# Latent tokens: both expert tables streamed once per latent step in place of gathered rows

## What is computed

```python
def peer_ffn(h, lp):
    q = (xt @ lp["peer_wq"]).reshape(n_tok, PEER_HEADS, 2, PEER_HALF)
    s = jnp.einsum("thmd,mhnd->thmn", q, lp["peer_keys"])
    v1, i1 = lax.top_k(s[:, :, 0], PEER_TOPK)
    v2, i2 = lax.top_k(s[:, :, 1], PEER_TOPK)
    ...
    idx = jnp.take_along_axis(cand_i, pos, axis=-1)    # i1 * 128 + i2, of 16384 experts
    g = jax.nn.softmax(top_s, axis=-1)
    act = jnp.einsum("td,thkd->thk", xb, u_tab[ib])
    return jnp.einsum("thk,thkd->td", jax.nn.gelu(act) * gb, v_tab[ib])
```

## Time and profile before

| | |
|---|---|
| median of 3 runs | 2433.51 us (2430.46 to 2434.32) |
| span of the profiled execution | 2689.8 us |
| TensorE, VectorE, ScalarE, GpSimd busy | 1510.1, 1524.4, 281.3, 1466.1 us |
| moved by DMA | 969.43 MB, mean 360 GB/s |
| granted TensorE clock, mean | 0.721 |

### The profile page before, as it was taken

How to read it: one execution, slowest core, us unless ns; L and a number is a source line. 1 busy time by engine, 2 the same in 40 slices (tenths; PEclk the granted TensorE clock), 3 DMA queues, 4 the chain that set the end, 5 groups by cost and what they waited for, 6 DMA issues and landing times.

```text
span 2689.8 us, 20637 instructions
## 1 busy us (share of the span) xinstructions
PE 1510.1 (56%) x6676; PEld 682.0 (25%) x6676; DVE 1524.4 (57%) x4059; ACT 281.3 (10%) x715; POOL 1466.1 (55%) x1540
## 2 busy tenths in 40 slices
PE   6898668694244554554556866868400444442466
PEld 2464433371012110122312442354100100110012
DVE  0349974756886555455360965575776844446401
ACT  1321133010000110100000032211000000000000
POOL 0005445536665666666556635545676666667664
PEclk8889888896666665676768787878755655565568
DMA  9979998988999999999979988888899999999997
GB/s 360 411 320 379 395 388 324 365 306 318 357 397 411 412 388 379 371 410 411 389 286 374 364 341 314 324 313 296 318 399 373 343 383 375 358 374 383 378 357 271
DMA packets 238044, 969.43 MB, mean 360 GB/s; under 512 B 26314, under 2 KB 28746, under 8 KB 227954
## 3 DMA queue, kind: packets, MB, share of 16 engines
q0 software_dynamic: 221184, 805.40, 78.0%
q1 hardware_dynamic: 16754, 162.71, 14.9%
HBM read 964.87 MB, written 3.15 MB: 360 GB/s over the span
## 4 chain that ended last, share of the span: by engine, by line
DVE 27%; PE 24%; issue 15%; POOL 13%; another core or an unknown queue 11%; DMA 7%; ACT 2%; SPq 0%; DVEq 0%; ACTq 0%; POOLq 0%
PE acc L1077 8%; PE psum L1031 6%; DVE ring L1871 6%; POOL work L695 6%; POOL ring L695 5%; DVE work L1871 3%; PE psum L786 3%; DVE work L1463 2%; POOL wring L695 2%; DMA ring<-peer_v_in,vidx 2%; PE psum L796 2%; DVE work L1460 2%; DMA ring<-peer_u_in,idx 1%; DVE wring L1871 1%
## 5 line engine op out<-in xcount | busy, mean ns | idle before, releaser
L695 POOL DMA_INDIRECT ring<-peer_u_in,idx x415 | 396.5, 955 | 460.6 <-DVE idx L1566 208.0
L1871 DVE CUSTOM_DVE_ANT_0 ring<-ring,h_kept 128x1024 f32<-128x1024 f32 x415 | 488.9, 1218 | 126.3 <-DMA ring<-peer_u_in,idx 93.5
L695 POOL DMA_INDIRECT ring<-peer_v_in,vidx x392 | 378.5, 966 | 325.8 <-PE acc L1077 116.9
L1077 PE MATMUL acc<-ring,vw 128*32 128x512 f32 x1412 | 299.2, 778 | 276.6 <-DVE vw L1852 107.6
L1077 PE MATMUL acc<-work,vw 128*32 128x512 f32 x852 | 218.4, 794 | 325.5 <-DVE vw L1852 155.0
L1871 DVE CUSTOM_DVE_ANT_0 work<-work,h_kept 128x1024 f32<-128x1024 f32 x220 | 262.0, 1219 | 159.3 <-DMA work<-peer_u_in,idx 124.2
L695 POOL DMA_INDIRECT work<-peer_v_in,vidx x267 | 252.0, 944 | 144.8 <-issue 74.0
L695 POOL DMA_INDIRECT work<-peer_u_in,idx x220 | 207.1, 941 | 116.7 <-issue 58.9
L1031 PE MATMUL psum<-work,wring 128*128 128x256 f32 (+1 forms) x896 | 187.1, 369 | 49.5 <-issue 46.6
L786 PE MATMUL psum<-wring,work 128*128 128x512 f32 (+1 forms) x432 | 180.4, 575 | 32.4 <-issue 22.8
L1031 PEld LDWEIGHTS psum<-work,wring 128*128 128x128 f32 x896 | 160.3, 216 | 81.5 <-issue 62.0
(11 more groups left out here) (244 smaller groups left out, 2028.4 us busy)
## 6 DMA issues: line engine op xcount, KB each, us to landing
wring<-w_in_in SPq DMA_DIRECT2D x17, 2048.0 KB
wring<-peer_wq_in SPq DMA_DIRECT2D x14, 2048.0 KB
wring<-mod_w_in SPq DMA_DIRECT2D x10, 2048.0 KB
ring<-mod_w_in SPq DMA_DIRECT2D x9, 2048.0 KB, 12.2
wring<-w_out_in SPq DMA_DIRECT2D x8, 2048.0 KB
work<-mod_w_in SPq DMA_DIRECT2D x5, 2048.0 KB, 14.4
ring<-peer_u_in,idx POOLq DMA_INDIRECT x415
ring<-peer_v_in,vidx POOLq DMA_INDIRECT x392
```

Source lines behind the costliest of these rows:

```text
L695: nc.gpsimd.indirect_dma_start(slots[slot_of[n]], None, table, bass.IndirectOffsetOnAxis(ap=at[:, col + r:col + r + 1], axis=0))\
L1077: ins = mm(acc[half][lane:lane + QUAD, :], w[:, at:at + QUAD], two[j - pair][0][:, half * CHUNK:(half + 1) * CHUNK], start=(r == 0), stop= ...
L1871: V.tensor_tensor_reduce(held, held, h_kept[:, :], 1.0, 0.0, ALU.mult, ALU.add, dots[:, dots_at(k, t) + r:dots_at(k, t) + r + 1]).then_inc ...
```

## The change

For the latent steps (k = 1 and 3) the gathers are replaced. For the context steps they stay.

1. `laid_out` gives both tables in a second layout: 64 parts of U and 64 of V per layer, each 128 partitions x 8 KB (1 MB). Expert n * 128 + m lies on "partition n, column m"; a part holds two columns m, so a pass covers 256 experts. The U part is transposed, so that its 128x128 blocks can be weights.
2. After the last `choose` of a latent step comes a new generator, `dense_gates`. Per tile, the picks' row numbers, column numbers and gates are transposed (`pickT`). Then, per group of four tokens, VectorE writes two one-hot matrices [128 picks, 128] (one weighted by the gates), TensorE multiplies them for each token into a 128x128 matrix of gates, and ScalarE carries them into a staging tile. After eight groups ScalarE sends the tile to the main memory (2 MB, eight times per step). The calculation of `idx` and the regrouping to `vidx` are left out for latent steps; `idx` and `vidx` hold the two halves as floats.
3. The events of a latent step are now `p`, `w`, `m`, 64 of each, and one `x`. `p`: GpSimd loads a part of U (direct DMA); TensorE multiplies 16 times (two columns of experts x 8 blocks, 256 moving columns: both tiles of tokens) into a bank; ScalarE applies gelu into one of 7 buffers. `w`: VectorE multiplies by the dense gates, of which GpSimd loads a slice of 1 MB every four passes. `m`: GpSimd loads a part of V; TensorE multiplies 8 times (two columns x two tiles x two halves of 512) into `acc` for tile 0 and `h_kept` for tile 1. `p` runs five passes ahead of `m`, `w` two.
4. 85% of these events are spread by weight over all pauses of the context step behind; the rest, and all of step 3's, come after the dense work. Nothing but the gates' own work is at the new pauses.
5. Parts use the ten places of the ring as five, and at the end four more in the weight ring. The lent places beside and behind the context layouts are gone, those of `hn`, `mod_g2` and `mod_norms` stay. `ahead` is off for all steps. Step 2 waits for the stores of the gates ahead of some of its buffers, where it waited for `picked`.

The sizes, and the loads on GpSimd:

```diff
+PAIR = 2
+PASSES = 128 // PAIR
+LEAD, READY = 5, 2
+SLOTS = 5
+SLICE = 4
+GROUP = 32
...
-                self.ahead = k == 3
+                self.ahead = False
...
+            def load_part(kind, k, c):
+                to, landed, _ = part(kind, k, c)
+                slot, n = part_at(kind, k, c), part_no[kind, k, c]
+                if n - part_first[k] >= part_slots(k):
+                    pool.wait_ge(*part_left(slot, k, n))
...
+                nc.gpsimd.dma_start(to, io["u_parts" if kind == "p" else "v_parts"][k // 2, c]).then_inc(landed, 16)
```

TensorE:

```diff
+            def dense_gates(st):
...
+                    for q in range(P // 4):
+                        p = job(pe, "G", k, t, q)
+                        pe.wait_ge(*after("hot", k, t, q))
+                        hot = st.L.onehot[q % 2]
+                        for u in range(4):
+                            ins = mm(p[:, u * P:(u + 1) * P], hot[:, u * P:(u + 1) * P], hot[:, 512 + u * P:512 + (u + 1) * P],
+                                     start=True, stop=True)
+            def experts(kind, k, c):
+                if kind == "p":
...
+                    for j in range(PAIR):
+                        for b in range(DB):
+                            ins = mm(p[:, j * 256:(j + 1) * 256], w[:, b, j * P:(j + 1) * P], st.L.hT[1][:, b, 0:256],
+                                     start=(b == 0), stop=(b == DB - 1))
...
+                    for j in range(PAIR):
+                        for t in range(2):
+                            for half in range(2):
+                                ins = mm(sum_of(t, half), w[:, j * 256 + t * P:j * 256 + (t + 1) * P],
+                                         rows_of[:, j, half * CHUNK:(half + 1) * CHUNK],
+                                         start=(c == 0 and j == 0), stop=(c == PASSES - 1 and j == PAIR - 1))
```

ScalarE:

```diff
+                        carry(stage.rearrange("p (n t) -> p t n", t=GROUP)[:, q % 8 * 4:q % 8 * 4 + 4, :],
+                              bank("G", k, t, q)[:, :].rearrange("p (t n) -> p t n", t=4), "G", k, t, q)
+                        if q % 8 == 7:
+                            act.wait_ge(*taken("G", k, t, q))
+                            act.dma_start(io["dense_gates"][st.layer, g], stage).then_inc(*mark(stored, k, g, n=16))
...
+                    A(acts[c % len(acts)], bank("act", k, c)[:, :], ACT.Gelu_apprx_tanh).then_inc(*take("act", k, c))
```

VectorE:

```diff
+                        for u in range(4):
+                            n = 4 * q + u
+                            d(V.tensor_scalar(hot[:, u * P:(u + 1) * P], c("count"), picks[:, n:n + 1],
+                                              picks[:, 2 * P + n:2 * P + n + 1], ALU.is_equal, ALU.mult))
+                        wide = [P, 4, P]
+                        V.tensor_tensor(hot[:, 512:1024].rearrange("p (u n) -> p u n", u=4), c("count").unsqueeze(1).broadcast_to(wide),
+                                        picks[:, P + 4 * q:P + 4 * q + 4].unsqueeze(2).broadcast_to(wide), ALU.is_equal)\
+                            .then_inc(*mark("hot", k, t, q))
...
+                    V.tensor_tensor(w, w, g[:, first:first + PAIR, :, :], ALU.mult).then_inc(*mark("wt", k, c))
```

The plan:

```diff
+def expert_events(st):
+    events = []
+    for c in range(-LEAD, PASSES):
+        for kind, at in (("p", c + LEAD), ("w", c + READY), ("m", c)):
+            if 0 <= at < PASSES:
+                events.append((kind, st.k, 0, at))
+    return events + [("x", st.k, 0, 0)]
...
+BESIDE_SHARE = 0.85
...
         elif k and k < len(steps):
-            dots = max(n for n, event in enumerate(left) if event[0] == "u") + 1
-            most = dots + int((len(left) - dots) * ROOM)
-            spread(plan, part(names[0][0], ("wq", 3)), left[:dots])
-            spread(plan, part(("ps", 0), ("exp", 0)), left[dots:most])
+            most = int(len(left) * BESIDE_SHARE)
+            spread(plan, names, left[:most])
             plan[None] = left[most:]
```

More of the change, by code:

```diff
@@ L344, in mod_column @@
             return columns_of[:, at:at + 1]
-        def dots_at(k, t):
-            return (sum(st.T for st in steps[:k]) + t) % 2 * PICKS
-        vw_places = [held[:, :] for held in vw] + [region(16384 + i * CHUNK, CHUNK) for i in range(2)]
         def vw_of(k, t, q):
-            return vw_places[q % (4 if k == STEPS - 1 else 2)]
+            return vw[q % 2][:, :]
         def job(pe, *key):
@@ L471, in spare @@
             slots.extend(views)
[L473 to L488, removed]
         lent = len(slots)
@@ L516, in build_pass, with part_slots, part_at, part @@
             used_after[key] = counts[key[0]]
+        g_slices = [region(12336 + i * 2048, 2048) for i in range(2)]
+        acts = [hn[t][:, i * CHUNK:(i + 1) * CHUNK] for t in range(2) for i in range(2)]
+        acts += [region(16432 + i * CHUNK, CHUNK) for i in range(3)]
+        parts = [ring[:, i * PAIR * D:(i + 1) * PAIR * D] for i in range(SLOTS)]
+        parts += [held[:, i * PAIR * D:(i + 1) * PAIR * D] for held in wring for i in range(2)]
+        def part_slots(k):
+            return len(parts) if k == STEPS - 1 else SLOTS
+        def part_at(kind, k, c):
+            return (part_no[kind, k, c] - part_first[k]) % part_slots(k)
+        part_filled, seen_in = {}, {}
+        for key in part_no:
+            slot = part_at(*key)
+            seen_in[slot] = seen_in.get(slot, 0) + 1
+            part_filled[key] = 16 * seen_in[slot]
+        def part(kind, k, c):
+            return parts[part_at(kind, k, c)], part_landed[part_at(kind, k, c)], part_filled[kind, k, c]
+        def part_left(slot, k, n=len(part_no)):
+            kind, k, c = max((key for key in part_no if key[1] == k and part_no[key] < n and part_at(*key) == slot), key=part_no.get)
+            return full("act", k, c) if kind == "p" else after("summed", k, c)
+        def slice_no(k, n):
+            return (k // 2 * (PASSES // SLICE) + n) // 2 + 1
+        def sum_of(t, half):
+            return acc[half][:, :] if t == 0 else h_kept[:, half * CHUNK:(half + 1) * CHUNK]
         def used_by(kind, n):
@@ L1169, in opening @@
                 yield "start"
+                if st.first and k:
+                    act.wait_ge(*after("g_stored0", k - 1, 6))
+                    act.wait_ge(*after("g_stored1", k - 1, 7))
                 if st.first:
@@ L1562, in choose, with index @@
                 yield ("choose", t, 6)
-                at = (st.X + t) * PICKS
+                if not st.lat:
+                    yield from index(st, t, part, half_f, picks)
+                if part == 0:
+                    return
+                yield from weigh(st, t)
+            def index(st, t, part, half_f, picks):
+                k, at = st.k, (st.X + t) * PICKS
                 d(V.tensor_scalar(half_f[0], half_f[0], float(P), float(st.layer * EXPERTS), ALU.mult, ALU.add))
@@ L1631, in dense @@
                         .then_inc(*mark("par_lam", st.layer))
+                if st.first and k:
+                    dve.wait_ge(*after("g_stored0", k - 1, 6))
+                    dve.wait_ge(*after("g_stored1", k - 1, 7))
                 d(V.memset(st.L.xraw[:, :, 0:2], 0.0))
@@ L1956, in pauses_of @@
         names += [(("exp", t), 2)]
+    if st.lat:
+        names += [(("gates", t, i), 2) for t in range(T) for i in range(5)]
     return names
@@ L2037, in gather_plans @@
         plan = {}
-        def part(first, last):
-            return names[labels.index(first):labels.index(last) + 1]
         if k and k < len(steps) and steps[k].T == 2:
```

281 lines of the change are left out of this document (201 added, 80 removed).

## The result

The kernel with the change takes 3188.34 us in the median (3186.01 to 3190.81), the kernel before 2433.51: a ratio of 1.311, 95% interval 1.309 to 1.313. It is slower by 755 us. The prediction was 3265 us, range 3050 to 3480.

What follows compares the result with a forecast made beforehand. Latent gathers bound by bytes now, TensorE at full clock after, gates exposed: 705 + 105 + 1051 + 510 + 105 + 903 = 3379 us of profile; with 0.905 on 705 and 510 only, 3265 us, range 3050 to 3480.

Steps and rivals of the forecast that it cites:

- TensorE's price of a pass: Latent experts: 32 records at 0.216 us and 16 at 0.43, 13.8 us a pass, 883 us per latent step.
- Rival 3: Experts' stages: short waits between passes keep TensorE's clock at 0.8, 1104 us per step, total 3707; 7%.
- Rival 1: Experts' passes: TensorE streams denser than the trace rows, 10.9 us a pass, total 2893; 4%.
- The factor 0.905: Median over profiled span, 2433.51 to 2689.8 us, read as recording being slower; applied only to stages set by bytes.
- The two scaled stages: Before the first gates (705) and latent 1 beside context 1's gathers (510), set by bytes: 1100 us after 0.905.
- The four unscaled ones: Both gates' stages, context 1 with experts, and the end: 2164 us, kept unscaled as TensorE's rate sets them.
- the 28 us put for the lost opening ahead and the fewer places: Latent 1 beside context 1's gathers: 18 for tile 0 not prepared ahead, 10 for only ten ring places.
- the unscaled sum of 3379: Whole kernel in profile time, all stages summed with no factor for the median: 3379 us.
- The gates: Dense gates after each latent step's last choice: 64 groups at 1.6 us, 105 us with turnings, covered by nothing.
- Context 1: Context 1 with latent 0's experts: 883 experts, 125 dense work, 35 waits, 8 adding to x, 1051 us.
- The other engines in a pass: Experts' passes: VectorE, ScalarE and GpSimd work lies beside 13.8 us of TensorE and costs nothing; 145 GpSimd issues.
- Supply of instructions (rival 4): TensorE short of instructions, 30 to 60 us; or context 1 and experts cover worse, up to 150 more; together 12%.

Runs made afterwards that it cites:

- half_bytes: Changed kernel loading only the first half of each U and V part, used for both expert columns, same matmuls: 3191.69 us, ratio 1.312.
- half_u: Changed kernel with U's products taking only four of the eight feature blocks, no bytes removed: 2754.35 us.
- half_width: Changed kernel with the latent experts' matmuls in fp16 instead of fp32, same bytes read from main memory: 2095.42 us, ratio 0.862.
- before_again: Kernel before, unchanged, recorded once more: 2431.21 us, span of the recorded execution 2429.3 us.
- the set at 2700: Changed kernel, unchanged, run again where the kernel before took 2705.11 us: 3334.94 us, ratio 1.230.
- experts_behind: Changed kernel with all 64 expert passes of latent step 1 after context 1's dense work, none beside it: 3401.08 us.
- half_width_b: The changed kernel with fp16 experts, run again where the kernel before was slower: 2243.19 us, ratio 0.827.
- half_width_gates: Changed kernel with fp16 experts, plus one-hot matrices, staging tiles and stored gates in fp16: 2269.43 us, ratio 0.842.
- half_width_onehot: Changed kernel with fp16 experts and fp16 one-hot matrices, staging tiles and stored gates left fp32: 2218.49 us, ratio 0.820.

## Why the prediction was right, and where it wasn't

**TensorE's price of a pass: right.** 13.8 us from two spacings in the trace of before; 13.8 measured. It carries the verdict: 883 us per latent step in the place of about 700 us of DMA time. half_bytes and half_u show both sides of it.

**The clock: right.** Rival 3 (0.8) gave 3707; the mean is 0.99 in both stages, in which TensorE hardly pauses. Rival 1 falls with the spacing: U's records still start every 0.216 us and V's every 0.43; the 0.3 us that it took for V stands in no row and in no run. Of the two rules of the Trainium skill (TensorE: Matmul & The Clock Gate, Back-to-back issue gap) the isolated gap, 2 x 216 ns, agrees with the 0.43 us between V's records, and with half_width, where V's fp16 records of 512 columns start 0.43 us apart in pairs, so 0.215 us each. The sustained 131 ns for 512 columns shows nowhere here. The page of the Trainium skill on precision (FP8 and Floating Point Precision, TensorE Precision Notes) says that true fp32 takes four passes through the array; half_width agrees, with 1.91 us for U in place of 7.07 and 0.215 us for a matmul of V in place of 0.86.

**The factor 0.905: wrong in its reason.** I read the gap between span and median as the cost of being recorded. before_again has a span of 2429.3 us at a time of 2431.2. The rows came from an execution with slow gathers, the median from a set at 2432. The choice to put the factor on the stages with gathers alone was the right one for the wrong reason. And it wasn't one factor: from the set at 2700 to the one at 2432 the changed kernel's first stage goes by 621 / 694 = 0.895, the stage of step 3 by 400 / 484 = 0.826.

**Where the 77 us too many come from, and luck.** The two scaled stages were put at 1100 us and took 621 + 400 = 1021. The four unscaled ones were put at 2164 and took 122 + 1014 + 126 + 901 = 2163, but that is luck: the gates were 38 us longer than put, context 1 37 us and the end 2 us shorter. Of the scaled stages the one of step 3 missed most, 461 us for 400. Here the factor was worth 39 us (482 x 0.905 = 436, where before_again has 397), and the 28 us put for the lost opening ahead and the fewer places another 22: the stage took 400 us for 397, and 484 where the earlier trace rows have 482. The loss was next to nothing.

**The sum on its own ground.** With gathers as slow as in the rows, in the set at 2700, the unscaled sum of 3379 stands against 3334. Term by term, predicted and measured: up to the gates 705 and 694; gates 105 and 122; context 1 with experts 1051 and 1014; step 3 510 and 484; gates 105 and 122; the end 903 and 898.

**The gates: mis-sized by 17 and 21 us.** A group takes 1.62 us on VectorE where nothing holds it, as put (1.6), and 64 of them with their turnings 110 us, for 105. What was left out is ahead of them: each of the two gates' stages also holds the last gathered rows of the context and its adding to x. 11 us pass between the last gates at 621 and the first group at 632.0 us; in step 3, where the final norm of the context comes in too, it is 16 us, from 2157 to 2172.5. VectorE's two forms:

```profile
L2030 DVE TENSOR_SCALAR work<-const,work 128x128 f32<-128x128 f32 x512 | 143.6, 351 | 9.8 <-ACT work L1243 6.5 <-PE psum L1136 2.9 <-DVE x L2144 0.2
L2033 DVE TENSOR_TENSOR work<-const,work 128x512 f32<-128x512 f32 x128 | 89.0, 695 | 0.0
```

233 us for 128 groups are 1.8 us of busy time each, in which neighbours overlap. The idle time in front of them is 9.8 us in both steps together, most of it for the turned picks (L1243), so VectorE is the limit, as said.

**Context 1: over-sized by 37 us.** Dense work 125 and waits 35 were put. TensorE is idle only 1014 - 999 = 15 us in the stage: 11 us of waits for ScalarE and VectorE, where 35 were put, and 4 while x is added to. 64 passes at 13.78 us are 882 of the 999, so the dense work took some 117, for 125. So the waits were the mis-sized term. The dense work itself was 135 us at a mean clock of 0.80 in experts_behind, and is about 117 us here, at 0.99.

**The other engines in a pass: right.** No group of the experts' matmuls waited for any of them (GpSimd has 128 parts and 16 slices to issue per step, 144 and not 145).

**Supply of instructions (rival 4): not seen.** The two slow stretches of the earlier trace rows have no like in the experts' stages; TensorE's longest wait in context 1 is 2.7 us, ahead of the adding to x.

## What to carry to other kernels

Fewer bytes gain nothing when they are bought with matmuls that take longer than the bytes did. Price the new engine's work by the spacing of the same form of instruction in a full-clock stretch of the trace, before counting what the old one is rid of. Here 100 MB less per layer came with 883 us of fp32 matmuls. If the form is right and the engine too slow, look at the width of its operands: in fp16 the same change is 14% faster than the kernel before. And where a profile's span and the median of the runs are 10% apart, the two are of different conditions: profile once more before scaling one to the other.

## What the hardware showed that was not expected

- The same kernel before took 2432 us in some sets of runs and 2695 to 2705 in others, 11% apart, while the runs of one set lie within 1.2%. The difference is in the stages with gathers of 4 KB rows (nearly all of it: the first stage of the kernel before, with hardly a gather, took 276 and 269 us); stages with loads of 8 KB per partition and matmuls take the same time in both (the end stage of the fp16 version, from the end of the gates, 382 and 383 us). Whether it is the chip, and what in the gathers is slower, wasn't shown.
- A ScalarE copy of 128x512 from PSUM took 0.6 us written side by side and 2.68 us written as fp16 at steps of 64 bytes. In fp32 at steps of 128 bytes it was 1.07 us: the 208 such rows of the changed kernel average 0.885 us, of which 80 are of the first kind.
- VectorE's product of 128x512 took 0.69 us with fp32 gates and fp16 weights, and 0.42 us with both in fp16 (half_width_b and half_width_gates).
- The fp16 one-hot matrices made TensorE's own part of the gates cheaper, and its granted clock fell with it. In half_width_b it is busy 79 of 120 us at a mean of 0.91, in half_width_onehot 42 of 109 us at 0.52. VectorE is the limit in both, so the time wasn't hurt:

```profile
692.00:801.00 109.00, 42.19 (x283) 23.76 (x280) 104.33 (x332) 69.36 (x71) 2.36 (x5) 0.52 0.45 163
```
